# The third mixer's 31-tap convolution, computed in two phases of 512 tokens instead of one pass over 1024

## The reference, cut to what matters

```
def conformer_conv_branch(z_val, z_glu, z_gate, conv_w, conv_b, cn_g, cn_b, w_pw2, b_pw2):
    v = z_val * jax.nn.sigmoid(z_glu)
    y = lax.conv_general_dilated(
        v, conv_w[:, None, :].astype(v.dtype),
        window_strides=(1,), padding=[(CONV_K - 1, 0)],
        dimension_numbers=("NWC", "WIO", "NWC"),
        feature_group_count=W_CONV) + conv_b.astype(v.dtype)
    y = jax.nn.silu(group_layer_norm(y, cn_g, cn_b, CONV_GROUPS))
    y = y @ w_pw2.astype(y.dtype) + b_pw2.astype(y.dtype)
    return y * jax.nn.silu(z_gate)
```

## Time and profile before

| | us |
|---|---|
| median of 3 runs | 3774.49 (3773.03 to 3779.23) |
| the profiled execution | 3777.17 |
| its span | 3775.1 |
| PE busy in the span | 3596.8 (95%) |
| DVE busy | 2277.2 (60%) |
| ACT busy | 1669.5 (44%) |
| POOL busy | 464.2 (12%) |

### The profile page before, as it was taken

One profiled execution on the slowest core, in us unless ns is written; L12 is line 12 of the kernel. 1 busy time (PEld: TensorE's weight loads), 2 busy tenths in 40 slices (PEclk: granted clock), 3 DMA queues, 4 the chain that ended last, 5 costly groups with the idle time before them and its releaser, 6 DMA issues.

```text
span 3775.1 us, 46097 instructions
## 1 busy us (share of the span) xinstructions
PE 3596.8 (95%) x19070; PEld 2977.3 (79%) x19070; DVE 2277.2 (60%) x3007; ACT 1669.5 (44%) x2122; POOL 464.2 (12%) x373
## 2 busy tenths in 40 slices
PE   8999989999998898999999989999999999989998
PEld 6778868888876687877777758878777888868898
DVE  4445354356667675655655663577889887854432
ACT  4333244431114444467676772145555554542132
POOL 0001032200000121200000000012222232210001
PEclk9999999999999899999999999999999999999999
DMA  3012023342212011011111123121111111153111
GB/s 111 23 40 90 26 81 109 107 164 89 90 69 90 23 34 40 17 51 34 31 34 29 34 87 140 38 86 34 45 45 40 54 53 45 34 186 138 45 41 66
DMA packets 221237, 244.70 MB, mean 65 GB/s; under 512 B 10008, under 2 KB 177893, under 8 KB 221029
## 3 DMA queue, kind: packets, MB, share of 16 engines
q1 hardware_dynamic: 216247, 224.92, 18.5%
q10 hardware_dynamic: 4781, 16.84, 1.2%
HBM read 191.40 MB, written 50.33 MB: 64 GB/s over the span
## 4 chain that ended last, share of the span: by engine, by line
PE 79%; DVE 10%; ACT 6%; issue 3%; DMA 1%; POOL 0%; ACTq 0%; DVEq 0%; SPq 0%; POOLq 0%
PE pd L211 65%; PE pq L211 12%; PE pd L366 2%; DVE t L328 1%; DVE t L3541 1%; PE pq L366 1%; DVE t L3549 1%; ACT t L3122 1%; ACT t L320 1%; DVE t L3986 1%; DVE t L2456 0%; DMA yc_scratch<-t 0%; DVE t L3971 0%; DMA ym_scratch<-t 0%; DVE t L2084 0%
## 5 line engine op out<-in xcount | busy, mean ns | idle before, releaser
L211 PE MATMUL pd<-t 128*128 128x512 f32 (+2 forms) x13984 | 2891.4, 367 | 39.4 <-ACT t L3737 8.7
L211 PEld LDWEIGHTS pd<-t 128*128 128x128 f32 x13984 | 2349.6, 191 | 513.4 <-issue 93.2
L211 PE MATMUL pq<-t 128*128 128x128 f32 (+5 forms) x3750 | 632.0, 330 | 63.5 <-DVE t L4022 16.6
L211 PEld LDWEIGHTS pq<-t 128*128 128x128 f32 (+2 forms) x3750 | 480.4, 181 | 175.7 <-issue 33.3
L320 ACT ACTIVATE t<-t 128x2048 fp32r<-128x2048 f32 (+3 forms) x133 | 212.8, 1600 | 614.8 <-PE pd L211 578.5
L328 DVE TENSOR_TENSOR t<-t 128x2048 fp32r<-128x2048 f32 (+3 forms) x133 | 257.4, 1935 | 174.0 <-ACT t L320 173.5
L1923 DVE TENSOR_TENSOR t<-pd,t 128x512 f32<-128x512 f32 x256 | 172.8, 689 | 103.3 <-PE pd L211 101.2
L3245 DVE COPY t<-pd 128x512 f32<-128x512 f32 x64 | 44.2, 691 | 216.6 <-PE pd L366 216.6
L3549 DVE SCALAR_TENSOR_TENSOR t<-t 128x1024 f32<-128x1024 f32 x120 | 173.1, 1443 | 0.5
L3541 DVE SCALAR_TENSOR_TENSOR t<-t 128x1024 f32<-128x1024 f32 x120 | 170.4, 1420 | 2.1
L3938 POOL TENSOR_TENSOR t<-t 128x512 f32<-128x512 f32 x56 | 97.9, 1749 | 593.8 <-ACT t L3882 295.0
(11 more groups left out here) (346 smaller groups left out, 2804.3 us busy)
## 6 DMA issues: line engine op xcount, KB each, us to landing
t<-in_w_in_dram SPq DMA_DIRECT2D x97, 512.0 KB, 4.1
t<-in_w_out_dram SPq DMA_DIRECT2D x20, 1024.0 KB, 5.1
t<-in_w_in_dram SPq DMA_DIRECT2D x16, 1024.0 KB, 5.4
t<-in_w_mlp_dram SPq DMA_DIRECT2D x64, 256.0 KB, 3.7
u_scratch<-t SPq DMA_DIRECT2D x64, 256.0 KB, 3.8
t<-in_w_mlp_dram SPq DMA_DIRECT2D x16, 1024.0 KB, 4.9
t<-u_scratch SPq DMA_DIRECT2D x15, 1024.0 KB, 7.1
t<-in_x_dram SPq DMA_DIRECT2D x16, 512.0 KB, 8.4
```

The source lines that it names most:

```text
L211: ins = e.matmul(out, l, r, start=(first and j == 0), stop=(last and j == n - 1), skip_group_check=True)
```

## The change

Tokens are split into even and odd ones. `Pad` becomes two rows of 528: row 0 and row 1 hold the even and the odd places of the padded input, so that L3529's successor writes its 512 products alternately to the two rows. With E and O the tap sums over the even-numbered and the odd-numbered taps, one set of outputs is E + O of the same place, and the other is a third sum, of the added rows (`cX`) with the added taps (`cws`, taps 2j and 2j+1), less E one place on and less O. That is (a + b)(c + d) - ac - bd for ad + bc. So a block has

- one add for `cX`, 527 wide;
- 16 even taps, 513 wide (`conv_even`: one `tensor_scalar`, 15 `scalar_tensor_tensor`);
- 15 odd taps, 512 wide (`conv_odd`: one and 14);
- one add for the first outputs, written with a stride of two, and one difference `cQ`;
- 16 taps of the added weights over `cX`, 512 wide, in place in `cQ`; the last writes the other outputs with a stride of two.

These are 50 DVE instructions where there were 31. `dve_conv_a` has 20 steps instead of 17, `dve_conv_b` 15 as before; the weight in `mix_stage` stays 32. At the start of the stage four small DVE instructions form the added taps and twice the bias, and POOL has one more memset. The other engines' lists are the same but for that.

```diff
-    Pad = ring(ph, 1, [128, S + 30])
+    Pad = ring(ph, 1, [128, 2, 528])
...
+    cE, cO, cQ, cX = sbt(ph, [128, 513]), sbt(ph, [128, 512]), sbt(ph, [128, 512]), sbt(ph, [128, 527])
+    cws, cb32 = sbt(ph, [128, 128]), sbt(ph, [128, 8])
...
+    def tap_sum(j, g):
+        return cws[:, 8 * j + g:8 * j + g + 1]
...
+    def conv_even(e, g, j):
+        x = Pad.of("cpad", g)[:, 0, j:j + 513]
+        if j == 0:
+            for th in range(2):
+                e.wait_ge(*at["cin", g, th])
+            e.tensor_scalar(cE[:, :], x, taps(0, g), None, MUL).then_inc(*at.inc("dve", "ceven", g))
+        else:
+            e.wait_ge(*at["ceven", g])
+            e.scalar_tensor_tensor(cE[:, :], x, taps(2 * j, g), cE[:, :], MUL, ADD).then_inc(
+                *at.inc("dve", "ceven", g))
+
+    def conv_odd(e, g, j):
+        x = Pad.of("cpad", g)[:, 1, j:j + 512]
+        if j == 0:
+            e.tensor_scalar(cO[:, :], x, taps(1, g), pc("cb3", g), MUL, ADD).then_inc(*at.inc("dve", "codd", g))
+        else:
+            e.wait_ge(*at["codd", g])
+            e.scalar_tensor_tensor(cO[:, :], x, taps(2 * j + 1, g), cO[:, :], MUL, ADD).then_inc(
+                *at.inc("dve", "codd", g))
...
     def dve_conv_a(e, g):
...
-            e.tensor_tensor(p[:, 30 + th * 512:30 + th * 512 + 512], PD.of("cval", g, th)[:, :],
-                            Hs.of("csig", g, th)[:, :], MUL).then_inc(
+            at_ = 15 + 256 * th
+            e.tensor_tensor(p[:, :, at_:at_ + 256].rearrange("p r m -> p m r"),
+                            PD.of("cval", g, th)[:, :].rearrange("p (m r) -> p m r", r=2),
+                            Hs.of("csig", g, th)[:, :].rearrange("p (m r) -> p m r", r=2), MUL).then_inc(
                 *at.inc("dve", "cin", g, th, free=("cval", g, th)))
             at.also("dve", ("csig", g, th))
         yield
+        for th in range(2):
+            e.wait_ge(*at["cin", g, th])
+        e.tensor_tensor(cX[:, :], p[:, 1, 0:527], p[:, 0, 1:528], ADD).then_inc(*at.inc("dve", "cboth", g))
+        conv_even(e, g, 0)
+        yield
+        for j in range(14):
+            conv_odd(e, g, j)
+            if j % 2 == 0:
+                yield
+            conv_even(e, g, j + 1)
+            if j < 8 or j % 2:
+                yield
+
+    def dve_conv_b(e, g):
         a = e.take(Acc3, "cacc", g)
+        conv_odd(e, g, 14)
+        conv_even(e, g, 15)
+        yield
+        at.also("dve", ("cpad", g))
+        e.wait_ge(*at["ceven", g])
+        e.wait_ge(*at["codd", g])
+        e.tensor_tensor(a[:, 0::2], cE[:, 0:512], cO[:, :], ADD).then_inc(*at.inc("dve", "cy0", g))
+        e.scalar_tensor_tensor(cQ[:, :], cE[:, 1:513], cb32[:, g:g + 1], cO[:, :], SUB, ADD).then_inc(
+            *at.inc("dve", "ctaps", g))
+        yield
+        e.wait_ge(*at["tap_sums"])
+        e.wait_ge(*at["cboth", g])
+        for j in range(16):
             e.wait_ge(*at["ctaps", g])
+            e.scalar_tensor_tensor(a[:, 1::2] if j == 15 else cQ[:, :], cX[:, j:j + 512], tap_sum(j, g), cQ[:, :],
+                                   MUL, ADD if j else SUB).then_inc(*at.inc("dve", "ctaps", g))
+            if j > 2:
+                yield
```

More of the change, by code:

```diff
@@ L3533, in dve_conv_a @@
         yield
-        a = e.take(Acc3, "cacc", g)
         for th in range(2):
             e.wait_ge(*at["cin", g, th])
-        e.tensor_scalar(a[:, :], p[:, 0:S], taps(0, g), pc("cb3", g), MUL, ADD).then_inc(*at.inc("dve", "ctaps", g))
+        e.tensor_tensor(cX[:, :], p[:, 1, 0:527], p[:, 0, 1:528], ADD).then_inc(*at.inc("dve", "cboth", g))
+        conv_even(e, g, 0)
         yield
-        for k in range(1, 16):
-            e.wait_ge(*at["ctaps", g])
[L3541 to L3552, removed]
+        for j in range(14):
[6 more added lines that the diff above has]
+    def dve_conv_b(e, g):
+        a = e.take(Acc3, "cacc", g)
+        conv_odd(e, g, 14)
[11 more added lines that the diff above has]
+        for j in range(16):
+            e.wait_ge(*at["ctaps", g])
+            e.scalar_tensor_tensor(a[:, 1::2] if j == 15 else cQ[:, :], cX[:, j:j + 512], tap_sum(j, g), cQ[:, :],
+                                   MUL, ADD if j else SUB).then_inc(*at.inc("dve", "ctaps", g))
+            if j > 2:
+                yield
     def pe_conv_tail(e, g):
@@ L3652, in pool_mix_setup @@
     def pool_mix_setup(e):
-        e.memset(Pad.tiles[0][:, 0:30], 0.0).then_inc(*at.inc("pool", "pad3"))
+        e.memset(Pad.tiles[0][:, :, 0:15], 0.0).then_inc(*at.inc("pool", "pad3a"))
+        e.memset(Pad.tiles[0][:, 0, 527:528], 0.0).then_inc(*at.inc("pool", "pad3"))
         for l, w_ in enumerate(LV):
@@ L3669, in pool_mix_setup, with dve_tap_sums @@
         e.memset(At[:, :, :], 0.0).then_inc(*at.inc("pool", "At0"))
+    def dve_tap_sums(e):
+        w0 = PC[:, col["cw3a"]:col["cw3a"] + 128].rearrange("p (j s g) -> p j s g", j=8, s=2)
+        w1 = PC[:, col["cw3b"]:col["cw3b"] + 112].rearrange("p (j s g) -> p j s g", j=7, s=2)
+        e.tensor_tensor(cws[:, 0:64].rearrange("p (j g) -> p j g", j=8), w0[:, :, 0, :], w0[:, :, 1, :], ADD).then_inc(
+            *at.inc("dve", "tap_sums0"))
+        e.tensor_tensor(cws[:, 64:120].rearrange("p (j g) -> p j g", j=7), w1[:, :, 0, :], w1[:, :, 1, :],
+                        ADD).then_inc(*at.inc("dve", "tap_sums1"))
+        e.tensor_copy(cws[:, 120:128], PC[:, col["cw3b"] + 112:col["cw3b"] + 120]).then_inc(
+            *at.inc("dve", "tap_sums2"))
+        e.tensor_scalar(cb32[:, :], PC[:, col["cb3"]:col["cb3"] + 8], 2.0, None, MUL).then_inc(
+            *at.inc("dve", "tap_sums"))
     def dve_mix_setup(e):
+        dve_tap_sums(e)
         e.memset(eps3[:, :], 1e-6).then_inc(*at.inc("dve", "eps3"))
```

## The result

The changed kernel takes 3793.24 us, the median of 4 runs (3792.17 to 3797.93), against 3775.08 (3773.03 to 3779.23) for the kernel before beside it: ratio 1.0052, 95% interval 1.0039 to 1.0065. It is slower by 15 to 25 us. The profiled execution has a span of 3792.4 us where before had 3775.1.

A forecast was written before the change was run, and what follows sets the result against it. PE is 79% of the chain, DVE 10%; DVE binds from the last L4022 to PE's restart. Terms 6.3 + 3.2 - 1.0 = +8.5, less 0.5, give +8: 3782.5 us from 3774.5; own range 3776 to 3791, 8-in-10 3765 to 3798.

The forecast's parts named there:

- rival C: Narrow DVE operations cost more than their rows say, 0.1 us each in the binding half: 3803 us; chance 0.15.
- Step 4: DVE's binding half, rounds 1 to 3: more operations before L328 and first L3986, restart 3.3 us late, net +2.1 each.
- The surplus from POOL: DVE taps beside POOL products: 34 us of lengthening over the stage, assumed unchanged by the new form.
- Steps 6 and 9: Rounds 4 to 6: DVE's waits absorb delay, net nothing; clock: longer sigmoid waits slow rounds 2 and 3, 1.6 us each.
- Step 3: Between the L4022 pair and last L4022, two narrow taps replace two wide: 1.2 us gained in each of seven rounds.
- Step 2: Input products L3529 writing two phases: 0.69 us each as before; even doubled, 1.4 us a block more costs nothing.
- Steps 5, 7 and 8: Round 0 loses PE's 1.08 us wait, -1.0; round 7 nothing; centring waits L3576, 1.4 us a round, stay.
- The costs of the narrow operations: On DVE, a 512-wide tap takes 739 ns, 0.65 us start to start; about 36.5 us a block against 39.5.
- A: Rival: binding-half delay mostly taken up, POOL's path not binding and no clock drop, +1.7: 3776 us; chance 0.25.
- B: Rival: the binding half gets shorter, the sixteen operations before L328 costing what five did, -13: 3761 us; chance 0.10.
- The forecast's condition for being wrong: PE's sigmoid waits, forecast to reach about 4 us in rounds 1 to 3; no growth would make Step 4 wrong.

The follow-up runs named there:

- experiment 1: Changed kernel with ten narrow taps per block moved from between the last L4075 and L328 to ahead of the round's scan and L4071: 3748.11 us.
- experiment 3: Kernel before, its wide taps bunched as in the changed kernel, eight instead of five between the last L4022 and L328: 3799.71 us.
- experiment 5: Changed kernel with two narrow taps wherever the kernel before has a wide one, sums kept in place: 3770.50 us.
- Experiment 4: Changed kernel with POOL's power L619 put ahead of the pair of products it stood behind: 3785.06 us.
- experiment 6: Changed kernel with ten narrow taps moved ahead of the scan, plus the pair before the last L4075 moved behind it: 3744.56 us.
- experiment 7: Changed kernel with input products L3555 written from contiguous columns, without even/odd sorting (output not the reference's): 3792.11 us.

## Why the prediction was right, and where its size was off

It said slower, by 8 us, with waits for the sigmoid in place of waits for the state chain; measured are 18 us of that kind. So the way and the mechanism were right and the size was not: 3793.2 us lies above the range that the forecast gave itself, 3776 to 3791, and inside 3765 to 3798 only because that range made room for rival C. The two traces, aligned at PE's waits, give its terms one by one. In the table "restart" is the time from a round's state wait to the restart, "clock" what the stretch from there to the centring grew by. The kernel before has these rows in round 4:

```profile
2943.96 0.71 PE L211 MATMUL pq<-t 128*128 128x128 f32 x4 [2.66 <-DVE t L4022]
3002.93 5.74 PE L211 MATMUL pd<-t 128*128 128x512 f32 x24 [0.32 <-ACT t L3737]
3019.92 1.16 PE L211 MATMUL pq<-t 128*128 128x128 f32 x8 [1.39 <-DVE t L3576]
3052.51 0.71 PE L211 MATMUL pq<-t 128*128 128x128 f32 x4 [2.00 <-DVE t L4022]
```

and the one after:

```profile
2948.31 0.71 PE L211 MATMUL pq<-t 128*128 128x128 f32 x4 [0.81 <-DVE t L4075]
...
3028.84 1.16 PE L211 MATMUL pq<-t 128*128 128x128 f32 x8 [1.39 <-DVE t L3615]
3060.22 0.71 PE L211 MATMUL pq<-t 128*128 128x128 f32 x4 [0.81 <-DVE t L4075]
```

So in round 4 the restart is 3009.21 - 2948.31 = 60.9 us behind the state wait and was 59.0; from there to the centring it is 19.6 and was 17.0; and the way from the centring to the next state wait is 31.4 and was 32.6.

| term | predicted | measured |
|---|---|---|
| round 0 | -1.0 | -0.8 |
| PE at the last L4075, seven rounds | -8.4 | -10.9 |
| restart, rounds 1 to 3 | +9.9 | +12.6 (4.5, 4.1, 4.1) |
| restart, rounds 4 to 6 | +3.6 | +7.2 (1.9, 3.3, 1.9) |
| clock, rounds 1 to 3 | +3.2 | +3.1 |
| clock, rounds 4 to 6 | 0 | +5.6 (2.6, 1.3, 1.6) |
| round 7 | +1.1 | +2.1 |
| sum | +8.4 | +18.9 |

The measured sum is 18.8 by the centring waits of rounds 0 and 7 as well. Ahead of the stage the profiled execution after was 3.1 us quicker and behind it 1.7 slower, which makes the 17.3 us between the spans; these 3.1 us lie in code that the change leaves alone. The same code varies by more: in the nine profiled executions of this document the wait for the first sigmoid of the stage, 3.03 to 3.04 us each time, ends between 2501.4 and 2508.1 us.

**Step 4, what stands ahead of L328 and the first merge**, is right in its mechanism: experiments 1, 3 and 5 move nothing but the taps' places and give 3748, 3800 and 3771 us. 5.85 us late was predicted at the first merge, 6.1 came. The way back is where its size was off. It had L624 4.9 us late and 1.1 regained before the next front. L624 came 5.4 late (32.2 against 26.8), since POOL gained nothing on the way (its L619 began 5.6 late, as did the front that releases it), and it took 1.07 us longer. The front behind it was 4.6 to 5.0 late instead of 3.8, and the restart 4.1 to 4.5 instead of 3.3. Experiment 4 shows the price of this place: 1.6 us a round.

**The surplus from POOL, "kept whole"**, is the term of the cost model that failed. Above their undisturbed lengths (739 and 685 ns, L624 1221) the operations between 2495 and 3380 us lost 34 us on taps and 4 on fronts before; after it is 25 on taps, 21 on fronts and 7 on L624, so 53 instead of 38. (Taps after: 128 x 0.085 + 232 x 0.060; fronts: 56 x 0.146 + 56 x 0.227; L624: 7 x 1.066.) Meeting by meeting, the kernel before has 54 DVE operations that a POOL product makes longer, by 39.7 us together, and the one after 62, by 53.5. The loss of one is not fixed. In the nine traces it is what is left of the product that holds the DVE operation up, counted from the operation's start, less 0.12 to 0.20 us, whatever the operation's own length: after, 0.38 us on a sum that starts 0.57 before the product ends, 1.06 to 1.08 at 1.21 to 1.24, 1.32 on a front at 1.45. The Trainium skill, SBUF — State Buffer (SBUF: two separate sides), has it so, for a DVE instruction with two inputs in SBUF beside a GpSimd one that reads SBUF: whichever starts first has the shared ports for its whole length, an exclusive lock, and the other is blocked. The trace agrees: 0.74 to 1.80, 0.68 to 1.76, 1.21 to 2.28 us, and POOL's product at 2.23 us where L624 was first. So keeping the sum constant had no ground: the number of meetings and who starts first go by the order, and I did not ask which operation stands there when the later fronts release POOL. In experiment 5, with the taps back in the old places, L4023 and L4025 (the fronts) are at 725 and 729 ns: the meetings depend on the order. Their sum doesn't decide the time by itself, though: experiment 3 loses 37.7 us in them and takes 3800 us, experiment 6 loses 42.2 and takes 3745. What counts is a loss in the binding half.

**Steps 6 and 9, rounds 4 to 6**, hold the largest miss. I let the two waits for PE in the binding half take up the delay. They did at first (3.7 late behind the first, as predicted 3.5), but L624 came 4.7 us late in round 5 instead of 4.1, its longer run and the fronts beside POOL added to it, and the restart was 3.3 late instead of 1.2. The 1.2 was worked out for round 5; rounds 4 and 6 were 1.9 late. The wait for the sigmoid became 3.65 us in all three, not 1.5: in rounds 4 and 6 PE had a slow group behind its state wait before and has none now, and so it is there 1.4 us sooner. With that wait came what I had charged to rounds 2 and 3 alone: a group at the lower clock. Length, PE busy, granted clock, DMA share and GB/s of one such stretch, of the changed kernel and of experiment 1:

```profile
3009.00:3018.00 9.00, 8.79 (x30) 0.68 0.10 41
```

```profile
2981.00:2989.00 8.00, 7.69 (x36) 1.00 0.16 66
```

0.68 of full speed over the stretch is a part at 1.2 GHz instead of 2.4. Of the 45 us between the changed kernel and experiment 1, from the centring of round 0 to that of round 7, some 10 are these groups.

**Step 3** gained more than I said, 1.85 us in rounds 1 to 4 and 1.2 in rounds 5 to 7, since the surplus of 0.66 us that I kept at this spot is gone: the product of POOL that caused it (L3993, 2636.54 to 2637.81) now ends while DVE waits for PE, before the first of the two narrow taps starts at 2637.98. In rounds 5 to 7 it had not been there before either. **Step 2** is right in its time and wrong in its premise: L3555 takes 1.07 us instead of 0.69, and experiment 7 shows that this costs nothing. **Steps 5, 7 and 8** hold within 1 us; L3615's 11.1 us did not change at all. **The costs of the narrow operations** were right one by one: 0.74 us alone, 0.66 start to start. That DVE's busy time came out as expected, 19.4 us lower where 15 to 25 were, is luck. It holds 14 us more lost to POOL and 6 more for L3555, so the rest fell by some 39 us and not by 24; the 36.5 us a block of the prediction add up own lengths (46 x 0.74), though neighbours overlap by 0.08.

**The rivals.** A fails: the delay was not taken up and the clock did fall. B fails for the change as it stands, though its condition, a shorter binding half, is what experiments 1 and 6 make true, and these give 27 to 30 us, not 13. C's 3803 us is about as far from the measured time as the forecast's 3782.5, and its reason is wrong: a narrow tap costs 0.66 us start to start where 0.65 was put, and 0.03 more was its condition. The forecast's condition for being wrong ("if the waits for the sigmoid do not grow") was not met.

## What to carry to other kernels

A change that splits instructions also changes how many of them a weaving step holds, and where the engine is in step with another only once a round, the place of the work is worth more than its amount: the same instructions gave 3793, 3771, 3748 and 3745 us here, and the old ones 3800, 3774 and 3752. Before judging a new form, put it in the old places; then fill the hole that the trace shows in front of the engine's long wait. When a path is late, look at what it will then run beside: an operation that becomes late enough to start together with the neighbour's next one pays for the neighbour too (L624 here, 1.07 us a round).

## What the runs showed of the hardware that was not expected

- Of the taps, sums, fronts and L624 in the nine traces 462 were held up by a POOL product, and each lost what was left of the product, less 0.12 to 0.20 us, whatever its own length: 1.06 us on a tap of 0.74, 1.08 on a front of 0.68, 1.07 on a product of 1.21. Cutting a tap in two takes nothing off that loss; another order changes the number of cases (37 to 62) and their sum (28 to 54 us).
- The other way round, a POOL product that comes while narrow taps stand back to back can be kept out until they are over. In experiment 5 the product behind each state wait took 5.2 to 7.0 us where 1.27 is its length alone, in experiment 7 12.8 us in rounds 1 to 3 against 1.41 for the same product in the changed kernel; among wide taps the longest took 3.5. The time did not follow (3792 and 3793 us for the last two), and PE's timeline has no wait for POOL there.
- A DVE product whose output is written to two rows alternately, with inputs read in order, took 1065 ns; the same with contiguous pieces 687. The last of a block's sums and the add L3582, which write with a stride of two floats into one row, showed no such factor: 733 to 751 ns and 672 to 689 where no POOL product ran beside them.
- The slow groups behind a PE wait are not a smooth function of the wait. At 24 matmuls of 5.74 us: at the restarts of these kernels no group was slow after waits of 1.25 us and less; after 1.92 us one took 7.35; after 2.64 us 5.74, after 2.79 us 8.56 and 7.38; after 3.6 us 5.74 (once) to 8.50; after 4.7 us 8.12 and 8.52; after 5.2 to 6.3 us 7.1 to 8.4. The waits of 1.92 us and more cost up to another 2.8 us here, and what decides which of them do is not settled by these runs. Ahead of a half that DVE binds the loss is hidden (behind L4022), at the restart it is not.
